# Starting places of the split weights within 128 bytes of SBUF, stepped by 16 bytes from tile to tile, in a one-core float32 transformer step

## The reference

```python
def swiglu(x, w_in, w_out):
    a, gate = jnp.split(x @ w_in, 2, axis=-1)
    return (jax.nn.silu(a) * gate) @ w_out

def run_trunk(x, pos, h0_re, h0_im, k_past, v_past, pos_past, w):
    ...
    for l in range(DEPTH):
        if l == N_A:
            k_sh, v_sh = shared_kv(x, pos, w['attn_w_kv'])
        x = layer_norm(ALPHA * x + 0.5 * swiglu(x, w['ffn_w_in'][l, 0], w['ffn_w_out'][l, 0]), g[0], b[0])
        ...
        x = layer_norm(ALPHA * x + y, g[1], b[1])
        x = layer_norm(ALPHA * x + 0.5 * swiglu(x, w['ffn_w_in'][l, 1], w['ffn_w_out'][l, 1]), g[2], b[2])
```

## Time and profile before

| | |
|---|---|
| time, median of 2 runs | 2348.43 us (2346.33 to 2350.52) |
| time of the profiled execution | 2352.45 us |
| span of the profiled execution | 2350.6 us |
| PE busy, mean granted clock | 2257.9 us (96%), 0.987 |
| LDWEIGHTS busy | 2215.2 us (94%) |
| DVE, ACT, POOL busy | 1519.6 (65%), 1155.4 (49%), 581.1 us (25%) |
| weight-tile matmuls | 14,976 of 17,067 |
| DMA | 391 MB, 166 GB/s on average |

### The profile page before, as it was taken

The page is one execution under the profiler, slowest core; times in us unless marked ns, Lnnn a source line. Parts: engine busy times, 40 slices in busy tenths (PEclk is TensorE's granted clock), DMA queues, the critical chain, the costliest instruction groups (busy, mean ns, idle before and its releaser), DMA issues. The chain is left out here.

```text
span 2350.6 us, 42458 instructions
## 1 busy us (share of the span) xinstructions
PE 2257.9 (96%) x17067; PEld 2215.2 (94%) x17067; DVE 1519.6 (65%) x2284; ACT 1155.4 (49%) x1947; POOL 581.1 (25%) x499
## 2 busy tenths in 40 slices
PE   8999999999998998999999999999999999899997
PEld 8989999999998998999999999999999998889997
DVE  6888768656788677444474575655677665465444
ACT  4445543555644556433355465655466554354332
POOL 3256401123210253111251123011352011142110
PEclk9999999999999999999999999999999999999999
DMA  9567676454665455555569655544556456355552
GB/s 249 167 185 225 183 217 187 123 170 135 201 214 169 126 168 149 183 149 149 147 187 288 187 159 172 153 122 138 146 156 189 134 150 185 108 146 162 145 155 79
DMA packets 702292, 391.11 MB, mean 166 GB/s; under 512 B 25001, under 2 KB 689042, under 8 KB 702098
## 3 DMA queue, kind: packets, MB, share of 16 engines
q1 hardware_dynamic: 662720, 332.44, 49.3%
q10 hardware_dynamic: 39378, 55.96, 7.0%
HBM read 366.53 MB, written 21.82 MB: 165 GB/s over the span
## 5 line engine op out<-in xcount | busy, mean ns | idle before, releaser
L473 DVE TENSOR_TENSOR wl<-raw,wh 128x1024 fp32r<-128x1024 f32 (+1 forms) x640 | 795.2, 1243 | 469.0 <-ACT wh L467 467.2
L489 PE MATMUL tile_ps<-xh,wh 128*128 128x256 f32 (+1 forms) x3520 | 1056.8, 300 | 29.1 <-DVE wl L473 16.4
L490 PE MATMUL tile_ps<-xl,wh 128*128 128x256 f32 (+1 forms) x3520 | 1038.6, 295 | 0.0
L491 PE MATMUL tile_ps<-xh,wl 128*128 128x256 f32 (+1 forms) x3520 | 1038.2, 295 | 0.0
L467 ACT CAST wh<-raw 128x1024 fp32r<-128x1024 f32 (+1 forms) x640 | 655.4, 1025 | 753.0 <-PE tile_ps L491 743.7
L489 PEld LDWEIGHTS tile_ps<-xh,wh 128*128 128x128 f32 x3520 | 668.6, 190 | 39.1 <-DVE wl L473 21.0
L490 PEld LDWEIGHTS tile_ps<-xl,wh 128*128 128x128 f32 x3520 | 668.4, 190 | 1.0 <-issue 0.2
L491 PEld LDWEIGHTS tile_ps<-xh,wl 128*128 128x128 f32 x3520 | 668.5, 190 | 0.0
L605 POOL TENSOR_TENSOR hl<-hf,hh 128x256 fp32r<-128x256 f32 (+1 forms) x176 | 247.9, 1408 | 1285.4 <-ACT hh L531 1284.8
L489 PE MATMUL tile_ps<-hh,wh 128*128 128x320 f32 (+1 forms) x1472 | 444.0, 302 | 12.8 <-POOL hl L605 10.2
L490 PE MATMUL tile_ps<-hl,wh 128*128 128x320 f32 (+1 forms) x1472 | 433.7, 295 | 0.0
(11 more groups left out here) (295 smaller groups left out, 1773.9 us busy)
## 6 DMA issues: line engine op xcount, KB each, us to landing
raw<-in_ffn_w_in_dram SPq DMA_DIRECT2D x352, 512.0 KB, 3.8
raw<-in_ffn_w_out_dram SPq DMA_DIRECT2D x128, 448.0 KB, 3.6
raw<-in_ffn_w_out_dram SPq DMA_DIRECT2D x64, 512.0 KB, 3.9
raw<-in_ssm_w_glu_dram SPq DMA_DIRECT2D x32, 512.0 KB, 3.8
raw<-in_attn_w_kv_dram SPq DMA_DIRECT2D x32, 512.0 KB, 3.9
wt<-scr_w ACTq DMA_DIRECT2D x16, 512.0 KB, 4.2
cp<-scr_c ACTq DMA_DIRECT2D x16, 512.0 KB, 4.1
raw<-in_attn_w_q_dram SPq DMA_DIRECT2D x16, 512.0 KB, 3.7
```

The lines of the kernel that those rows point to most:

```text
L473: nc.vector.tensor_tensor(wl[n % WS][:, 0:k, :], raw[n % RAWS][:, 0:k, :], wh[n % WS][:, 0:k, :].bitcast(F32), ALU.subtract).then_inc(w_lo, 1)
L489: nc.tensor.matmul(o, wh[w][:, kk, :], xa, start=kk == 0, stop=False)
L490: nc.tensor.matmul(o, wh[w][:, kk, :], xb, start=False, stop=False)
L491: mm = nc.tensor.matmul(o, wl[w][:, kk, :], xa, start=False, stop=kk == ROWS[n] - 1)
```

## The change

The buffers of the split weights become 128 bytes longer each, and tile n uses a window in them whose start moves: the high part begins 16 * (n % 8) bytes in, the low part 16 * (n // 8 % 8) bytes in. In 64 tiles every pair of the two places comes once. raw, xh, xl, hh and hl keep their places within 128 bytes (what lies behind the weights moves up by 768 bytes, six times 128). Since that space was needed, two tables (skip) move to a place in the S5 region that is free by then, and fold and dw (two) move into the region of the prompt's V rows, which is only free once the prompt's attention is done; so DVE makes fold a little later.

```diff
-        wh = [keep(f"wh{s}", [P, KMAX, P], F32R) for s in range(WS)]
-        wl = [keep(f"wl{s}", [P, KMAX, P], F32R) for s in range(WS)]
+        whs = [keep(f"wh{s}", [P, KMAX * P + 32], F32R) for s in range(WS)]
+        wls = [keep(f"wl{s}", [P, KMAX * P + 32], F32R) for s in range(WS)]
...
+        def w_high(n):
+            lead = 4 * (n % 8)
+            return whs[n % WS][:, lead:lead + KMAX * P].rearrange("p (k m) -> p k m", m=P)
+
+        def w_low(n):
+            lead = 4 * (n // 8 % 8)
+            return wls[n % WS][:, lead:lead + KMAX * P].rearrange("p (k m) -> p k m", m=P)
...
-                nc.scalar.copy(wh[n % WS][:, 0:k, :], raw[n % RAWS][:, 0:k, :]).then_inc(w_hi, 1)
+                nc.scalar.copy(w_high(n)[:, 0:k, :], raw[n % RAWS][:, 0:k, :]).then_inc(w_hi, 1)
...
-                nc.vector.tensor_tensor(wl[n % WS][:, 0:k, :], raw[n % RAWS][:, 0:k, :],
-                                        wh[n % WS][:, 0:k, :].bitcast(F32), ALU.subtract).then_inc(w_lo, 1)
+                nc.vector.tensor_tensor(w_low(n)[:, 0:k, :], raw[n % RAWS][:, 0:k, :],
+                                        w_high(n)[:, 0:k, :].bitcast(F32), ALU.subtract).then_inc(w_lo, 1)
...
-            o, w = ps[:, n % PSS, 0:NT[h]], n % WS
+            o, wh, wl = ps[:, n % PSS, 0:NT[h]], w_high(n), w_low(n)
...
-                nc.tensor.matmul(o, wh[w][:, kk, :], xa, start=kk == 0, stop=False)
-                nc.tensor.matmul(o, wh[w][:, kk, :], xb, start=False, stop=False)
-                mm = nc.tensor.matmul(o, wl[w][:, kk, :], xa, start=False, stop=kk == ROWS[n] - 1)
+                nc.tensor.matmul(o, wh[:, kk, :], xa, start=kk == 0, stop=False)
+                nc.tensor.matmul(o, wh[:, kk, :], xb, start=False, stop=False)
+                mm = nc.tensor.matmul(o, wl[:, kk, :], xa, start=False, stop=kk == ROWS[n] - 1)
...
-            V.tensor_tensor(fold[:, :], ident[:, 0:DEC], ident[:, DEC:P], ALU.add).then_inc(z_fold, 1)
             V.memset(vtok[DEC:P, 4, :], 0.0)
...
                     dve.wait_ge(s_o, 2 * ITEMS)
+                    V.tensor_tensor(fold[:, :], ident[:, 0:DEC], ident[:, DEC:P], ALU.add).then_inc(z_fold, 1)
                     for b in range(2):
                         V.memset(exS[b][:, PAST + DEC:], 0.0)
```

More of the change, by code:

```diff
@@ L267, in build @@
         prod = [am(f"prod{k}", [P, 4 * BLK * GC]) for k in range(2)]
+        skip = [am(f"skip{s}", [P, P]) for s in range(2)]
         assert am.at <= gm.at
@@ L284, in build @@
         rows2 = gm("rows2", [P, P])
-        skip = [gm(f"skip{s}", [P, P]) for s in range(2)]
         dtrow = gm("dtrow", [NPAIR, 2])
@@ L322, in build @@
         stz = km("stz", [P, 2, 8])
-        fold = km("fold", [P, DEC])
-        dw = [km(f"dw{s}", [P, DEC]) for s in range(2)]
         xa = Map(qa_at)
@@ L356, in build @@
         pTS = [xa(f"pTS{s}", [P, (PAST // P + 1) * DEC]) for s in range(2)]
+        fold = xa("fold", [P, DEC])
+        dw = [xa(f"dw{s}", [P, DEC]) for s in range(2)]
         assert xa.at <= v_at + 4 * 4 * D
```

## The result

The changed kernel takes 2363.89 us in the median of 2 runs (2362.23 to 2365.56) against 2348.43 us (2346.33 to 2350.52): the medians lie 15 us apart. The ratio on record is 1.0053, 95% interval 1.0032 to 1.0074, which is 12 us (8 to 17). The prediction was 2354 us with a range from 2305 to 2415 us.

What follows compares the result with a forecast made beforehand. TensorE was taken to bound the kernel through the distance between matmul starts. The profiled 2352.45 us plus 6 us for the weights' places gave 2358.5 us, or 2354 us as a median, with a range of 2305 to 2415 us.

Steps and rivals of the forecast that it cites:

- little change: Whole kernel: forecast, no effect at all, or DVE as bound; 2329 to 2364 us, chance 0.60.
- What bounds the kernel: TensorE sets the time, busy 96% of the span; what counts is how far apart its matmuls start.
- 256 columns: TensorE tile matmuls of this width: half of the possible loss of the quicker spacing, +6 us.
- the short state: 256-column matmuls starting 113.3 ns apart rather than about 117.6, lasting over many tiles; about 60% taken as long.
- the bound of +13 us: Cost if all 256-column matmuls went to the long spacing: 0.4 x 7488 x 4.3 ns.
- the old distance was a good one: TensorE: at some new distances streams meet more often, 13.3 or about 9 ns more each; 2411 us at three of eight; 0.26.
- 320 columns: TensorE tile matmuls of this width: 146.7 ns apart everywhere, held independent of addresses; no change taken.
- The collision rival: TensorE weight loads and operand reads collide at some distances, some 320-column matmuls 160 ns apart; slower, chance 0.26.
- the faster rival: TensorE: old distance was bad, 320-column tiles fall near 140 ns; up to 69 us gained, 2279 us; chance 0.14.
- The view modulo 128: Weights against moving operand: distance within 128 bytes was always 64 and now takes all eight multiples of 16.
- The rule on TensorE's two ports: Independent ports for operand and weights: by it no place could matter, and the places term would be 0.
- ACT and DVE, fold, skip: Weight splits at new places 0 (0 to +3 us), later fold 0 (-0.3 to +0.3 us), moved tables 0.

Runs made afterwards that it cites:

- e2: Changed kernel, but high and low parts both begin at 0 in even tiles and 128 bytes in odd ones; 2342.75 us, ratio 0.9966.
- e3: Changed kernel, but high and low parts always begin 16 bytes in; 2361.80 us, ratio 1.0044.
- e12: Changed kernel, but high and low parts always begin 32 bytes in; 2362.66 us, ratio 1.0049.
- e5: Changed kernel, but starts of 0 or 128 bytes bring all six weight buffers to 0 within 256 bytes; 2351.41 us, ratio 0.9997.
- e7: As e5, but weights for tiles on hh and hl lie at 128 within 256 bytes, giving them x's distance of 64; 2349.27 us, ratio 0.9991.
- e8: Kernel before with x's 64 spare bytes taken out, so weights and x share one place within 256 bytes; 2365.51 us, ratio 1.0060.
- e1: Changed kernel with both starting offsets held at 0; longer buffers, moved tables and later fold stay; 2345.05 us, ratio 0.9977.
- e11: Changed kernel, but fixed distances by width: 256 columns always high 64, low 192; 320 columns begin 64 bytes in; 2333.35 us, ratio 0.9927.

## Why the prediction was right, and where it was not

*The number.* Right by its range, and in part by luck. The forecast was +6 us and the change cost 12 to 15 us; 2363.89 us lies at the very upper end of the forecast's own range for little change (2329 to 2364 us). Its sign came from an argument that the runs do not bear out, and its size was half of a term or less.

*What bounds the kernel.* Right. Nearly the whole effect is in the distance between the starts of tile matmuls; PE's busy time moved with it in every run (2230.9 to 2276.9 us), and DVE's stayed between 1518 and 1522 us.

*256 columns.* Right in sign, wrong in size and in reason. This was the term of the sum that was mis-sized: +6 us, as half of the loss of the short state, where the table gives 15.4 + 1.4 = 16.8 us. That 60% of the matmuls were long was a good estimate (58% by the table). But the changed kernel has 11% short left and not half, and its mean is 118.2 ns, above the 117.6 ns taken for the long state, so that even the bound of +13 us was passed by 4 us. The reason that I gave, that a state is lost when every tile begins at another place, was wrong: e2 moves at every tile and loses nothing, e3 and e12 never move and lose all. One part of it holds: at (64, 64) a state does last from tile to tile, as the forecast had read from the earlier trace rows. What decides whether it can be had is the pair of distances. The old one for x, (64, 64), happened to have the short state, and most of the new ones do not. That is the rival "the old distance was a good one" in its mechanism, but at 256 columns only. Its price, a second full excess of 9 to 13 ns on the tiles hit, was too high: the bad places cost 3 to 5 ns.

*320 columns.* The term (0) was right within 1 us, the reason was not. I held the 146.7 ns to be independent of addresses, because x and hh agreed at different steps between groups and different addresses. The steps were in fact the same at 320 columns (1280 bytes for both), and the addresses differed by 128 bytes within 256, which does nothing there as long as high and low part have one distance (before, e5, e7, e8). In the changed kernel single tiles have means from 144.2 to 149.1 ns, which cancel out to 146.9; fixed pairs have 144.9 to 146.9. The collision rival's tiles at 160 ns and the faster rival's near 140 did not show. By its own test ("wrong if 320 columns took more than one value") this step fell.

*The view modulo 128.* The prediction and the change both counted distances within 128 bytes, and so said that all tile matmuls had one distance. e1 and e5 show that 128 bytes more or less are a difference (145.6 against 146.7 ns), and e7 that it had made x and hh differ.

*The rule on TensorE's two ports.* The Trainium skill, "TensorE: Matmul & The Clock Gate", step 1 of "Step-by-step: what each phase is for", says that loading the next weights takes no read bandwidth from the running matmul. What the prediction drew from it, that no place could matter and this part would be 0, did not hold: fixed places differ by up to 6 ns at 256 columns of float32r (114.0 in e11, 119.9 in e8). Whether the weight load takes reads from the matmul no trace shows, so the rule itself is left open. The 11 ns that the prediction held against the rule at 320 columns say nothing on it: the Trainium skill gives that formula, in "Back-to-back issue gap" on the same page, for a single matmul by itself, and says that in a stream of weight loads and matmuls both set the spacing. Nor do whole steps of 16 bytes make a good place: e3 and e12 keep to them and have the whole loss.

*ACT and DVE, fold, skip.* 0 was right: no wait of PE grew, and the layout by itself (e5, with everything moved as in the change) has a ratio of 0.9997. That fold became three times as long (0.76 us after 0.26) was not foreseen, but stayed hidden.

*What stays open.* Why just these pairs have these levels. The trace shows when matmuls start and not what held one back; that two reads of TensorE meet is an argument and not shown. All places that are multiples of 16 but not of 64 that were tried alone (16, 32) are bad at 256 columns; 48 was not tried alone, nor was x moved other than in e8, nor any distance beyond 256 bytes. There may be something beyond: in e1, with 320 columns of x, even and odd groups of a tile alternate between 146.2 and 144.9 ns, and their distances differ by 256 bytes. What puts the matmuls at (64, 64) into the short or the long state, in which they then stay, is not explained; since the share of short ones differed at this pair (55%, 62% and 63% in before, e5 and e7 for x), a part of before's time is chance.

## What to carry to other kernels

Where float32r matmuls run back to back with a weight load for each, compare the distance between their starts with the column count; if several ns are left over, sweep the starting bytes of weights and moving operand within 256 bytes, one fixed place at a time, since a run that steps through all of them only shows their mean. A pair at which the short state comes back within a tile is worth more than one that merely allows it. The best place depended on the width and on the pair of high and low part, and chosen by both it was worth 0.7% here without a single instruction more. A number that two cases share (146.7 ns) is not shown to be independent of what the two cases also share.

## What the runs showed of the hardware that I had not expected

- The same float32r matmuls of 256 columns start 113.3, about 117.7 or 120.0 ns apart, those of 320 columns 144.6 to 148 ns, as the places of weights and moving operand are chosen; at (64, 64) both 113.3 and 117.7 occur and last over tiles. The columns alone are 106.7 and 133.3 ns at the granted 2.4 GHz.
- A shift of 128 bytes matters (e1 against e5), though both places are the same within 128 bytes.
- With high and low part 128 apart and both at a multiple of 64, 320 columns are quicker than with both at one distance: 144.9 or 145.6 ns against 146.7. At odd multiples of 16 or 32 (e3, e12) the 128 bytes between them gain nothing (146.6 to 146.9).
- One addition of 128x64 on DVE took 0.26 us at its old place in the program and 0.76 us at the new one. In all twelve runs with the new place it ends 0.08 us after GpSimd's subtraction of hl, which was under way when it began, as if it had waited for that one; at the old place it ends 0.08 us after a copy on GpSimd (qd). No run takes GpSimd's instruction away, so the wait is not shown.
